# Eight-core two-layer hybrid backbone: second layer's conditioning pieces later, tokens in chained pieces, unread matmuls in all planned waits

## The chip, the cores and the metric

The kernel runs on the 8 cores of one Trainium2 chip. All cores run the same program, each on its own share of the tokens, with the same weights, and no core talks to another. The time is the device time of the slowest core in microseconds (us). Each core has TensorE (matmuls), VectorE, ScalarE, GpSimd and SyncE; DMAs are issued from GpSimd's queue (the pool queue) and from SyncE's.

## What is computed

Two layers over 2048 tokens a core: 1024 context tokens (4 sequences of 256) and 1024 latent tokens (one sequence). Layer 0 mixes with a bidirectional RG-LRU (a gated linear recurrence), layer 1 with a chunked token-mixing MLP; each is followed by a SwiGLU FFN (1024 to 2816 to 1024). Every norm is modulated by a shift and a scale, and every branch by a gate, computed from a conditioning vector:

```python
def adaln(cond, w, b):
    m = jax.nn.silu(cond) @ w + b          # w: (1024, 6 * 1024) per layer
    return m.reshape(cond.shape[0], N_MOD, D_MODEL)

for i in range(DEPTH):
    hp = rmsnorm(xp, norm_mix[i]) * (1.0 + mp[:, 1]) + mp[:, 0]
    op = mixer(hp)                          # RG-LRU in layer 0, chunk MLP in layer 1
    xp = xp + mp[:, 2] * op
    hp = rmsnorm(xp, norm_ffn[i]) * (1.0 + mp[:, 4]) + mp[:, 3]
    xp = xp + mp[:, 5] * swiglu(hp, ...)    # and the same for the latent tokens with ms
```

## The kernel before

**Tiling.** Tokens stand as columns, features on the partitions, in four tiles of 512 tokens: tiles 0 and 1 are context, 2 and 3 latent. A matmul is 128 x 128 weights against 512 tokens; eight of them over the 1024 features fill one PSUM bank. PSUM has 8 banks: `BF` hands out 0 to 3 in turn, `BM` 4 to 6, and bank 7 gathers the conditioning.

**The planner.** The program is first recorded as tasks (`Prog._add`, line 163) with an engine, a priority (lower goes first), a planned duration, the tasks that they depend on, and for DMAs a planned rate. `Prog.schedule` (line 211) is a list scheduler that simulates the five engines and writes one fixed order for each. `slack` is added to a task's planned end, so what depends on it is planned later; it costs nothing by itself. On the chip each engine goes through its list strictly in order, with semaphore waits where a task depends on another engine's: a matmul whose data are late holds up all that stand behind it. ScalarE's choice (line 236) adds a penalty for a task whose function needs another activation table: `SWP` = 12 for tasks with priority 1 or more, `URG` = 2 for those below.

**Unread matmuls.** `Prog.warm` (line 268) goes through the planned order of TensorE; in each planned gap of over 0.8 us that begins before `WARM` = 400 us it puts up to ten matmuls of 256 columns (`onesB` against `condT`), whose result nobody reads, into a free bank. They show in the trace as `pb<-condT,onesB`.

**Order of the work.** x tile 0 and layer 0's conditioning are loaded; `lru((0,))` is the recurrence of tile 0 over 8 chunks of 128 features, `out_proj` its output projection; then the FFN's group 0 for tile 0 runs interleaved with `lru((1,))` (priority `P1`), whose projection follows (`out_proj(0, ..., (1,), sp=OSP1)`: the first `sp` of 8 chunk matmuls of a bank as one task, the rest as another, so the first can go before the last chunks are done). While tile 1 is worked on, the space of x tiles 2 and 3 holds recurrence weights; afterwards both tiles are loaded (`load_x`, 2 MB each, on SyncE's queue), normed into h, and their space serves `lru((2, 3))` as scratch; behind it they are loaded again, in eight quarter loads on the pool queue (`XRP` = 3), for the residual of `out_proj` of tiles 2 and 3. Meanwhile `ffn(0, 0)` does FFN group 0 for tile 1, then groups 1 and 2 for tiles 0 and 1, at the lowest priority 5: it fills TensorE whenever nothing else is ready. Then come `ffn(0, 1)`, layer 1, and the final norms.

**FFN and conditioning pieces.** `ffn` (line 619) goes through groups of the 22 hidden chunks (8, 8, 6). For each pair of chunks it loads a gate and an up weight (1 MB each, read as f32, stored as bf16) through the four slots of `ringF`, and then four down weights. `mods` is a list of conditioning pieces: after each pair and after each down weight one is taken from it, with its load through the next slot of `ringF`. A piece (`mod_piece`, line 452) is 1 MB of weights (`modw`; layer 0's last ones come as `modc`) and four matmuls against `condT` into bank 7; after the last piece of a set `mod_final` transposes the sum and writes modT and amod, which norms and residuals read. Layer 0's later pieces are planned with 2 us of slack (`SLK`), layer 1's with none. `ffn(0, 0)` for tile 1 carries layer 1's first set (8 pieces), `ffn(0, 1)` the other 16.

Projection weights and `lru_in` pieces go through the three slots of `ringM`.

Of the kernel before, what the change touches and what calls it, by code (L numbers as in the profile page):

```python
# [13 lines left out]
KC = 8  # L14
# [121 lines left out]
SLK, URG = 2.0, 2.0  # L136
PN = 0
OSP, OSP1 = 6, 8
# [4 lines left out]
M4 = 0  # L143
XRP = 3
# [3 lines left out]
P1 = 0.8  # L148
# [4 lines left out]
WARM = 400.0  # L153
PRE = (5, 6, 9, 9, 4, 4, 4, 6)
TABLE_US = 1.28
# [196 lines left out]
def snapshot(ress):  # L352
    out = set()
    for r in ress:
        if r.w is not None:
            out.add(r.w)
        out.update(r.r)
    return list(out)
# [21 lines left out]
def emit_program(P, A):  # L380
# [71 lines left out]
    def mod_piece(l, G, kc, prio=None, ring=ringF):  # L452
# [6 lines left out]
        wv, wres = ring.load(desc, 1 << 20, prio=prio, slack=SLK if l == 0 and G > 0 else 0.0)  # L459
# [51 lines left out]
    def load_x(tt, extra=()):  # L511
        P.dma("sp", "xs%d" % tt, lambda e: e.dma_start(out=x_fm[:, tt], in_=A["d_xin"][tt]),
              wr=[XR[(m, tt)] for m in range(KC)], extra=extra, nbytes=2 << 20)

# [104 lines left out]
    def ffn(l, hf, extra=(), mods=(), ep=1, after=None, segs=((0, (0, 1)), (1, (0, 1)), (2, (0, 1))), kept=None):  # L619
# [16 lines left out]
        for grp, tls in segs:  # L636
            j0, j1 = FGROUPS[grp]
            nj = j1 - j0
            for jp in range(j0, j1, 2):
# [26 lines left out]
                if mods:  # L666
                    mod_piece(*mods.pop(0), prio=2)
# [18 lines left out]
            if last and tls == (1,):  # L686
                last_tile(2 * hf + 1, [dload(pi) for pi in range(4)], nj, BZ)
            else:
                for pi in range(4):
                    down(pi, tls, *dload(pi))  # L690
                    if mods:
                        mod_piece(*mods.pop(0), prio=2)
                if last:
                    after(2 * hf)
# [94 lines left out]
    GK6 = Res()  # L789
# [392 lines left out]
    load_x(2, extra=snapshot(KR[0:3] + [GK6]))  # L1182
    load_x(3, extra=snapshot(LR[4].all() if M4 else KR[3:6] + [GK6]))
# [11 lines left out]
    for tt in (2, 3):  # L1195
        if XRP == 0:
            load_x(tt, extra=xre)
            continue
        for q in range(4):
            P.dma("pool", "xq%d" % (4 * (tt - 2) + q), lambda e: e.dma_start(out=x_fm[:, tt, 2 * q:2 * q + 2, :], in_=A["d_xin"][tt][:, 2 * q:2 * q + 2, :]),  # L1200
                  wr=[XR[(2 * q, tt)], XR[(2 * q + 1, tt)]], extra=xre, nbytes=1 << 19, prio=XRP)
# [4 lines left out]
    ffn(0, 0, segs=((0, (1,)), (1, (0, 1)), (2, (0, 1))) if NSEG == 1 else ((0, (1,)), (1, (1,)), (2, (0, 1))), mods=[(1, 0, kc) for kc in range(KC)])  # L1206
# [198 lines left out]
```

How the kernel before makes its waits and increments, by code:

```python
    def then_inc(self, sem, n):  # L49
        self.call.append((sem, n))
        return self
# [57 lines left out]
    "dma_start": lambda e, a, k: e.dma_start(*a, **k),  # L109
    "matmul": lambda e, a, k: e.matmul(*a, **k),
    "memset": lambda e, a, k: e.memset(*a, **k),
    "scalar_tensor_tensor": lambda e, a, k: e.scalar_tensor_tensor(*a, **k),
    "tensor_copy": lambda e, a, k: e.tensor_copy(*a, **k),
    "tensor_reduce": lambda e, a, k: e.tensor_reduce(*a, **k),
    "tensor_scalar": lambda e, a, k: e.tensor_scalar(*a, **k),
    "tensor_tensor": lambda e, a, k: e.tensor_tensor(*a, **k),
    "tensor_tensor_scan": lambda e, a, k: e.tensor_tensor_scan(*a, **k),
    "transpose": lambda e, a, k: e.transpose(*a, **k),
    "wait_ge": lambda e, a, k: e.wait_ge(*a, **k),
}
def replay(calls, e):
    for c in calls:
        ins = PLAY[c[0]](e, c[1], c[2])
        for (sem, n) in c[3:]:
            ins.then_inc(sem, n)
# [187 lines left out]
    def emit(self, order, sems, dsems):  # L314
# [22 lines left out]
                        kn[k2] = v2  # L337
                if kn.get(key, 0) < val:
                    kn[key] = val
            if t.dsem is not None:
                dcount[t.dsem] += 16
                t.tok = (t.dsem, dcount[t.dsem])
                t.last.then_inc(dsems[t.dsem], 16)
            else:
                count[e] += 1
                t.tok = (e, count[e])
                t.last.then_inc(sems[e], 1)
            t.know = dict(kn)
            q[e].append(t.calls)
        return q
```

## Time and profile before

| | |
|---|---|
| time, median of 3 runs | 1532.39 us (1531.67 to 1532.84) |
| the profiled execution | 1532.15 us, span of its slowest core (6) 1530.6 us |
| spans of cores 0 to 7 | 1517.4, 1529.7, 1529.6, 1517.4, 1529.7, 1516.5, 1530.6, 1517.2 us |
| mean granted TensorE clock of the cores | 0.983 to 0.989 |
| busy, share of the span | TensorE 94%, VectorE 59%, ScalarE 43%, GpSimd 15% |
| DMA | 151.56 MB, mean busy share of the 16 engines on the pool queue 53.2%, on SyncE's 3.4% |
| chain that ended last | TensorE 79%, DMA 9%, ScalarE 5%, issue 4%, VectorE 3% |

All rows below are of core 6. Times are microseconds from the span's start. PE is TensorE's matmuls, PEld its weight loads, DVE VectorE, ACT ScalarE, POOL GpSimd, SPq SyncE's queue. `out<-in` names what an instruction writes and reads: `pb` is PSUM, `h` the normed tokens, `MS` the recurrence's output, `FS` the FFN's hidden part, `x_fm` the tokens, and `condT` the conditioning vectors. Most operations are recorded by one helper, so that their line (L110, L105, ...) says only their kind. In brackets behind an instruction stands the time that its engine was idle before it, and what ended that. Matmuls are pipelined, so a mean of 380 ns is the time of one from start to end; eight in a row take 1.73 us.

### The profile page before, as it was taken

The numbers are of one execution on the slowest core, as the hardware profiler recorded it, in microseconds if no ns is written. First come the engines' busy times: TensorE is split into PE (matmuls) and PEld (weight loads), VectorE is DVE, ScalarE is ACT, GpSimd is POOL, SyncE is SP. The second block draws the span as 40 slices with busy tenths as digits, with TensorE's granted clock in tenths as the row PEclk, the third lists the DMA queues.
The fourth block names the chain that finished last, engine by engine and source line by source line (L and its number), as shares of the span: only waits on it lengthen the run. The fifth ranks groups of instructions, "written<-read, shape, count | busy, mean of one in ns | idle before, by whom it ended". The sixth has DMA issues, their size and how long they took to land.

```text
span 1530.6 us, 20044 instructions; the slowest of 8 cores (1516.5 to 1530.6 us)
## 1 busy us (share of the span) xinstructions
PE 1437.0 (94%) x6971; PEld 661.7 (43%) x6971; DVE 906.6 (59%) x1316; ACT 650.6 (43%) x866; POOL 225.7 (15%) x377
## 2 busy tenths in 40 slices
PE   4978996899999999999999999999999999999997
PEld 2433443444444445444444444444444444444444
DVE  1578695458687646528863364538856447744446
ACT  2597996548888234632013032632125013201023
POOL 6011021135231210011111100011110000101000
PEclk9999998999999999999999999999999999999999
DMA  9998368499435873554646754353332535985303
GB/s 176 171 191 129 49 110 193 57 156 146 74 60 86 168 137 55 84 83 70 110 69 97 117 101 72 56 83 56 55 63 47 86 55 93 198 142 87 65 1 110
DMA packets 50182, 151.56 MB, mean 99 GB/s; under 512 B 5410, under 2 KB 11042, under 8 KB 49572
## 3 DMA queue, kind: packets, MB, share of 16 engines
q0 software_dynamic: 45312, 133.32, 53.2%
q1 hardware_dynamic: 4772, 16.96, 3.4%
q8 instruction: 58, 0.95, 0.3%
q14 instruction: 40, 0.33, 0.1%
HBM read 270.94 MB, written 8.42 MB: 183 GB/s over the span
## 4 chain that ended last, share of the span: by engine, by line
PE 79%; DMA 9%; ACT 5%; issue 4%; DVE 3%; POOL 0%; DVEq 0%; ACTq 0%; POOLq 0%
PE pb L110 78%; DMA ringF<-modw 4%; DMA x_fm<-lru_in 2%; ACT h L105 1%; ACT reg L105 1%; ACT L105 1%; DMA x_fm<-xin 1%; DMA ringM<-lru_in 1%; DMA ringF<-ffn_d 1%; DVE x_fm L112 1%; DVE tmpn L112 1%; DMA tff<-lru_w_out 0%; ACT FS L105 0%; ACT x_fm L105 0%; DMA ringM<-lru_w_out 0%
## 5 line engine op out<-in xcount | busy, mean ns | idle before, releaser
L110 PE MATMUL pb<-h,ringF 128*128 128x512 bf16 x2624 | 585.7, 380 | 1.8 <-DVE FS L116 0.9
L110 PEld LDWEIGHTS pb<-h,ringF 128*128 128x128 bf16 x2624 | 255.3, 98 | 311.6 <-issue 9.3
L112 DVE SCALAR_TENSOR_TENSOR x_fm<-pb,modT,x_fm 128x512 f32<-128x512 f32 (+1 forms) x264 | 192.5, 733 | 196.6 <-PE pb L110 191.1
L110 PE MATMUL pb<-FS,ringF 128*128 128x512 bf16 x1312 | 296.6, 383 | 5.0 <-DVE x_fm L112 2.4
L105 ACT ACTIVATE tff<-pb 128x512 f32<-128x512 f32 x176 | 104.8, 596 | 385.7 <-PE pb L110 385.4
L112 DVE SCALAR_TENSOR_TENSOR tff<-tff,pb 128x512 f32<-128x512 f32 x176 | 120.2, 685 | 167.4 <-ACT tff L105 167.3
L110 PEld LDWEIGHTS pb<-FS,ringF 128*128 128x128 bf16 x1312 | 128.5, 99 | 161.8 <-issue 14.5
L116 DVE TENSOR_TENSOR FS<-tff,pb 128x512 bf16<-128x512 f32 x176 | 120.4, 685 | 68.8 <-PE pb L110 65.9
L105 ACT ACTIVATE h<-x_fm 128x1024 bf16<-128x1024 f32 (+2 forms) x86 | 84.2, 994 | 141.0 <-DVE x_fm L112 134.8
L105 ACT ACT_TABLE_LOAD x84 | 107.8, 1283 | 76.9 <-PE pb L110 69.3
L110 PE MATMUL pb<-h,ringM 128*128 128x512 bf16 x548 | 124.1, 380 | 4.3 <-DMA ringM<-lru_in 3.3
L105 ACT ACTIVATE reg<-reg 128x1024 f32<-128x1024 f32 (+1 forms) x68 | 57.4, 855 | 122.9 <-DVE reg L116 108.2
L110 PE MATMUL pb<-MS,ringM 128*128 128x512 bf16 x472 | 105.5, 379 | 3.7 <-DMA ringM<-lru_w_out 2.2
L105 ACT ACTIVATE h<-tmpn,modT 128x512 bf16<-128x512 f32 x120 | 82.4, 716 | 56.7 <-DVE tmpn L112 55.3
L112 DVE SCALAR_TENSOR_TENSOR tmpn<-x_fm,amod,rstd 128x512 f32<-128x512 f32 x120 | 86.2, 747 | 16.4 <-ACT rstd L105 8.9
L110 PEld LDWEIGHTS pb<-h,ringM 128*128 128x128 bf16 x548 | 53.3, 98 | 70.2 <-issue 7.2
L110 PEld LDWEIGHTS pb<-MS,ringM 128*128 128x128 bf16 x472 | 45.7, 98 | 60.4 <-issue 6.7
L109 POOL DMA_DIRECT2D ringF<-ffn_g x45 | 24.6, 548 | 265.5 <-PE pb L110 265.1
L110 PE MATMUL pb<-reg,h 128*128 128x512 bf16 x256 | 60.2, 379 | 0.0
L109 POOL DMA_DIRECT2D ringF<-ffn_d x48 | 25.7, 536 | 222.6 <-PE pb L110 218.3
L116 DVE TENSOR_TENSOR reg<-reg 128x1024 f32<-128x1024 f32 (+1 forms) x48 | 52.8, 1108 | 6.5 <-ACT reg L105 5.9
L110 PE MATMUL pb<-h,x_fm 128*128 128x512 bf16 x212 | 51.0, 379 | 5.6 <-ACT h L105 2.6
(152 smaller groups left out, 1252.3 us busy)
## 6 DMA issues: line engine op xcount, KB each, us to landing
ringF<-ffn_g POOLq DMA_DIRECT2D x45, 512.0 KB, 5.7
ringF<-ffn_u POOLq DMA_DIRECT2D x45, 512.0 KB, 6.9
ringF<-ffn_d POOLq DMA_DIRECT2D x36, 512.0 KB, 7.1
ringF<-modw POOLq DMA_DIRECT2D x34, 512.0 KB, 8.1
x_fm<-xin SPq DMA_DIRECT2D x4, 2048.0 KB, 14.3
yout<-x_fm SPq DMA_DIRECT2D x12, 512.0 KB, 8.3
ringM<-lru_in POOLq DMA_DIRECT2D x20, 256.0 KB, 5.6
ringM<-lru_w_out POOLq DMA_DIRECT2D x19, 256.0 KB, 5.7
```

What stands on the lines that cost most here:

```text
L105: "activation": lambda e, a, k: e.activation(*a, **k),
L109: "dma_start": lambda e, a, k: e.dma_start(*a, **k),
L110: "matmul": lambda e, a, k: e.matmul(*a, **k),
L112: "scalar_tensor_tensor": lambda e, a, k: e.scalar_tensor_tensor(*a, **k),
L116: "tensor_tensor": lambda e, a, k: e.tensor_tensor(*a, **k),
```

## The change

Six settings and two places in the program change:

- `mfrom=MF` with MF = 1: `ffn(0, 0)` takes no conditioning pieces in group 0 and begins with them in group 1. `ffn(0, 1)` is as before.
- Layer 1's pieces are planned with `SL1` = 3 us of slack, where they had none.
- `OSP1` = 6, before 8: tile 1's output projection is split in 6 + 2 chunk matmuls.
- `P1` = 1.0, before 0.8: the priority of `lru((1,))`. No other task lies between the two numbers, but ScalarE's penalty for a change of table becomes 12 there, before 2.
- `X4` = 3: x tiles 2 and 3 are loaded both times by `load_x4` on SyncE's queue, in quarters of 512 KB, each of which waits for the one before to have landed; the quarters of tile 3 follow those of tile 2.
- `WARM` = 9e9: unread matmuls go into planned gaps of the whole program.

```diff
-OSP, OSP1 = 6, 8
+OSP, OSP1 = 6, 6
-P1 = 0.8
+P1 = 1.0
-WARM = 400.0
+WARM = 9e9
+MF, SL1 = 1, 3.0
+X4 = 3
@@ mod_piece
-        wv, wres = ring.load(desc, 1 << 20, prio=prio, slack=SLK if l == 0 and G > 0 else 0.0)
+        wv, wres = ring.load(desc, 1 << 20, prio=prio, slack=SL1 if l == 1 else SLK if G > 0 else 0.0)
@@ emit_program
+    def load_x4(tts, extra=()):
+        prev = list(extra)
+        for tt in tts:
+            for q in range(4):
+                t = P.dma("sp", "xs%d" % tt, lambda e: e.dma_start(out=x_fm[:, tt, 2 * q:2 * q + 2, :], in_=A["d_xin"][tt][:, 2 * q:2 * q + 2, :]),
+                          wr=[XR[(2 * q, tt)], XR[(2 * q + 1, tt)]], extra=prev, nbytes=1 << 19)
+                prev = [t]
@@ ffn, at both places
-                if mods:
+                if mods and grp >= mfrom:
                     mod_piece(*mods.pop(0), prio=2)
@@ first load of tiles 2 and 3
-        load_x(2, extra=snapshot(KR[0:3] + [GK6]))
-        load_x(3, extra=snapshot(LR[4].all() if M4 else KR[3:6] + [GK6]))
+        load_x4((2,), snapshot(KR[0:3] + [GK6]))
+        load_x4((3,), snapshot(LR[4].all() if M4 else KR[3:6] + [GK6]) + [P.tasks[-1]])
@@ second load of tiles 2 and 3
-        for q in range(4):
-            P.dma("pool", "xq%d" % (4 * (tt - 2) + q), lambda e: e.dma_start(...), wr=[...], extra=xre, nbytes=1 << 19, prio=XRP)
+        load_x4((2, 3), xre)
@@ second part of the FFN of tiles 0 and 1
-    ffn(0, 0, segs=..., mods=[(1, 0, kc) for kc in range(KC)])
+    ffn(0, 0, segs=..., mods=[(1, 0, kc) for kc in range(KC)], mfrom=MF)
```

## Rows read from the trace of the kernel before

**Rows 1.** The page, section 1: busy us, share of the span, instructions.

```profile
PE 1437.0 (94%) x6971; PEld 661.7 (43%) x6971; DVE 906.6 (59%) x1316; ACT 650.6 (43%) x866; POOL 225.7 (15%) x377
```

**Rows 2.** TensorE's waits, whole span: us in total, times, longest.

```profile
PE pb L110 <- DMA ringF<-modw: 21.0, 10, 14.7
PE pb L110 <- DMA MS<-modw: 17.4, 3, 15.8
...
PE pb L110 <- DMA ringM<-lru_w_out: 2.2, 2, 1.5
PE pb L110 <- DMA ringF<-ffn_d: 2.2, 1, 2.2
```

**Rows 3.** Windows: us, busy (instructions) per engine, granted clock, DMA share, GB/s.

```profile
243.00:260.00 17.00, 2.27 (x18) 1.31 (x17) 9.47 (x17) 8.00 (x9) 0.53 (x1) 0.66 1.03 217
260.00:283.00 23.00, 20.80 (x105) 10.45 (x104) 5.25 (x7) 9.56 (x10) 4.10 (x8) 0.95 0.68 106
283.00:297.00 14.00, 9.56 (x56) 5.46 (x55) 7.28 (x11) 8.22 (x12) 0.68 (x2) 0.88 0.29 39
297.00:345.00 48.00, 46.75 (x221) 20.35 (x222) 25.93 (x39) 26.03 (x41) 14.43 (x24) 1.00 0.81 128
```

**Rows 4.** TensorE in order of time, 239 to 268: start, us, instruction, idle before.

```profile
243.20 1.26 PE L110 MATMUL pb<-condT,onesB 128*128 128x256 bf16 x10
259.19 0.62 PE L110 MATMUL pb<-ringF,condT 128*32 128x512 bf16 x4 [14.73 <-DMA ringF<-modw]
259.74 3.94 PE L110 MATMUL pb<-condT,onesB 128*128 128x256 bf16 x24
263.52 1.89 PE L110 MATMUL pb<-h,onesB 128*128 128x512 bf16 x8
265.25 2.97 PE L110 MATMUL pb<-MS,ringM 128*128 128x512 bf16 x13
```

**Rows 5.** GpSimd in order of time: the request of 240.24.

```profile
240.24 0.53 POOL L109 DMA_DIRECT2D ringF<-modw  x1 [3.14 <-PE pb L110]
```

**Rows 6.** TensorE in order of time: the statistics after 624.

```profile
624.49 3.63 PE L110 MATMUL pb<-h,onesB 128*128 128x512 bf16 x16
```

**Rows 7.** VectorE in order of time: the last write of MS.

```profile
252.28 0.69 DVE L116 TENSOR_TENSOR MS<-reg,MS 128x512 bf16<-128x512 f32 x1
```

**Rows 8.** DMA issues from 230 to 260: KB each, median us to landing.

```profile
ringM<-lru_w_out POOLq DMA_DIRECT2D x2, 256.0 KB, 19.1
```

**Rows 9.** Windows behind 400, columns as in rows 3.

```profile
400.00:450.00 50.00, 47.52 (x221) 21.41 (x220) 37.19 (x40) 41.97 (x54) 18.38 (x18) 1.00 0.43 71
...
480.00:500.00 20.00, 17.12 (x76) 7.32 (x75) 15.15 (x15) 18.38 (x24) 2.12 (x5) 0.94 0.56 93
...
870.00:890.00 20.00, 16.33 (x74) 7.16 (x73) 6.74 (x13) 0.00 (x0) 2.74 (x6) 0.91 0.93 164
1300.00:1320.00 20.00, 17.80 (x75) 7.61 (x74) 17.22 (x24) 8.78 (x12) 2.65 (x5) 0.91 0.89 157
```

**Rows 10.** TensorE's waits from 300 to 900: total, times, longest.

```profile
PE pb L110 <- DMA ringF<-modw: 4.2, 6, 1.6
```

**Rows 11.** The two token loads issued at 230.5 and 230.9: time to landing.

```profile
DMA to landing us min/median/max: 12.0/16.8/21.6
```

**Rows 12.** DMA issues from 260 to 283.

```profile
ringM<-lru_w_out POOLq DMA_DIRECT2D x5, 256.0 KB, 4.6
```

**Rows 13.** DMA issues of the whole span: KB each, median us to landing.

```profile
yout<-x_fm SPq DMA_DIRECT2D x12, 512.0 KB, 8.3
...
x_fm<-xin POOLq DMA_DIRECT2D x8, 512.0 KB, 18.9
```

**Rows 14.** ScalarE's groups from 145 to 255: count, busy us, mean ns, idle before.

```profile
L105 ACT ACT_TABLE_LOAD x24 | 30.8, 1283 | 1.1 <-PE pb L110 0.5
```

**Rows 15.** The window 145 to 255, columns as in rows 3.

```profile
145.00:255.00 110.00, 95.01 (x469) 44.16 (x469) 85.39 (x144) 99.20 (x121) 16.30 (x28) 0.97 0.56 111
```

**Rows 16.** The group of unread matmuls, whole span: count, busy us, mean ns.

```profile
L110 PE MATMUL pb<-condT,onesB 128*128 128x256 bf16 x316 | 46.4, 292 | 7.3 <-ACT h L105 4.1 <-ACT MS L105 1.9 <-DVE modT L116 0.7
```

More of the change, by code:

```diff
@@ L617, in emit_program, with ffn @@
     BM = Banks([4, 5, 6])
-    def ffn(l, hf, extra=(), mods=(), ep=1, after=None, segs=((0, (0, 1)), (1, (0, 1)), (2, (0, 1))), kept=None):
+    def ffn(l, hf, extra=(), mods=(), ep=1, after=None, segs=((0, (0, 1)), (1, (0, 1)), (2, (0, 1))), kept=None, mfrom=0):
         mods = list(mods)
@@ L690, in ffn @@
                     down(pi, tls, *dload(pi))
-                    if mods:
+                    if mods and grp >= mfrom:
                         mod_piece(*mods.pop(0), prio=2)
@@ L1181, in emit_program @@
     P.prio = 1
-    load_x(2, extra=snapshot(KR[0:3] + [GK6]))
-    load_x(3, extra=snapshot(LR[4].all() if M4 else KR[3:6] + [GK6]))
+    if X4 & 1:
+        load_x4((2,), snapshot(KR[0:3] + [GK6]))
+        load_x4((3,), snapshot(LR[4].all() if M4 else KR[3:6] + [GK6]) + [P.tasks[-1]])
+    else:
+        load_x(2, extra=snapshot(KR[0:3] + [GK6]))
+        load_x(3, extra=snapshot(LR[4].all() if M4 else KR[3:6] + [GK6]))
     P.prio = PB
@@ L1194, in emit_program @@
     xre = snapshot(LR[5].all() + LR[6].all() + GWB)
[L1195 to L1198, printed above, removed]
-        for q in range(4):
-            P.dma("pool", "xq%d" % (4 * (tt - 2) + q), lambda e: e.dma_start(out=x_fm[:, tt, 2 * q:2 * q + 2, :], in_=A["d_xin"][tt][:, 2 * q:2 * q + 2, :]),
-                  wr=[XR[(2 * q, tt)], XR[(2 * q + 1, tt)]], extra=xre, nbytes=1 << 19, prio=XRP)
+    if X4 & 2:
+        load_x4((2, 3), xre)
+    else:
+        for tt in (2, 3):
+            if XRP == 0:
+                load_x(tt, extra=xre)
+                continue
+            for q in range(4):
+                P.dma("pool", "xq%d" % (4 * (tt - 2) + q), lambda e: e.dma_start(out=x_fm[:, tt, 2 * q:2 * q + 2, :], in_=A["d_xin"][tt][:, 2 * q:2 * q + 2, :]),
+                      wr=[XR[(2 * q, tt)], XR[(2 * q + 1, tt)]], extra=xre, nbytes=1 << 19, prio=XRP)
     out_proj(0, "d_lru_w_out", (2, 3), BM, ringM)
@@ L1205, in emit_program @@
     cm_setup(BM)
-    ffn(0, 0, segs=((0, (1,)), (1, (0, 1)), (2, (0, 1))) if NSEG == 1 else ((0, (1,)), (1, (1,)), (2, (0, 1))), mods=[(1, 0, kc) for kc in range(KC)])
+    ffn(0, 0, segs=((0, (1,)), (1, (0, 1)), (2, (0, 1))) if NSEG == 1 else ((0, (1,)), (1, (1,)), (2, (0, 1))), mods=[(1, 0, kc) for kc in range(KC)], mfrom=MF)
     ffn(0, 1, mods=[(1, G, kc) for G in (1, 2) for kc in range(KC)])
```

## The prediction

> **What bounds the kernel now.** I read the page first [rows 1]: TensorE is busy for 1437.0 us, 94% of the 1530.6 us span, no other engine for more than 59%. So the time is TensorE's work plus TensorE's idle time, and only two things can shorten it: less idle time (93.6 us) or a higher clock in the stretches where it was granted less than full. The list of TensorE's waits [rows 2] splits the idle time by cause: 17.4 us at the start for the first conditioning pieces (not touched), then 21.0 us for conditioning pieces in ringF, of which one wait alone is 14.7 us; the rest is many waits of 1 to 2 us. A table of windows [rows 3] puts that wait in place: from 243 to 260 TensorE is busy 2.27 of 17 us and the granted clock is 0.66 (a mean of the two levels, 1.2 and 2.4 GHz), while the DMA engines are full (1.03). From 297 on it is nearly full again (46.75 of 48 us). The order of TensorE's instructions there [rows 4] shows whose fault it is: ten unread matmuls at 243.20, nothing until 259.19, then four matmuls of a conditioning piece (ringF against condT), 24 more unread ones, statistics, and at 265.25 the output projection of token tile 1. The piece was requested at 240.24 [rows 5] and is of modw, not modc; layer 0's last pieces are all modc, so this is one of the second layer's first eight, whose first reader is the norm at 624.49 [rows 6]. It blocks the engine because its four matmuls were planned here and the engine takes its list in order.
>
> **Part 1, the second layer's first eight pieces later (mfrom=1, slack 3).** Eight groups of four matmuls and eight 1 MB reads leave group 0 of the FFN and go to group 1; none is removed. The wait of 14.73 us [rows 4] goes. What is late next? The projection needs the last chunk of the recurrence, written by VectorE at 252.28 + 0.69 = 252.97 [rows 7]. So the projection can start at 253.1 + 1.73 for the statistics that stood ahead of it (263.52 to 265.25) = 254.9 instead of 265.25: -10.4 us, at most -12.1 if the statistics lie in the wait. Its weights have to be there too: the two requested from 230 to 260 took 19.1 us to land [rows 8], the second, requested right behind the piece, until 260; the piece's own 1 MB was ahead of it in the pool queue, and its removal brings it forward. The matmuls of the moved pieces (0.4 us each) cost the same in their new place. That place is under the scans of tiles 2 and 3: four with the gate and up weights of group 1, where the DMA is busy 0.43 (400 to 450), and four with its down weights, up to about 525, where it is 0.56 and more [rows 9], against 0.81 where most of them stood (297 to 345, [rows 3]). They must be through by the norm at 624.49 [rows 6], and are with 100 us to spare.
>
> The second layer's pieces were planned with no slack. From 300 on TensorE waits 4.2 us for them, the longest 1.6 [rows 10], so that 3 us of planned slack covers each. I take -2.5, bounds -4 and +2 (a slot freed 3 us later makes the weight behind it later; there is one such wait today, for ffn_d, 2.2 us [rows 2]).
>
> **Part 2, OSP1 8 to 6.** The projection of tile 1 is cut in 6 + 2 chunk matmuls. The three weights that the ring holds allow 18 matmuls of 1.73 / 8 = 0.216 us, 3.9 us, of work before 253.0, two of them 2.6 us. Against that stands that weights arrive late. I take -1.5, bounds -3.9 and 0. Nothing is added but eight planned groups.
>
> **Part 3, tokens in chained pieces.** The two 2 MB loads issued at 230.5 landed after 12.0 and 21.6 us [rows 11]; beside them a projection weight took 19.1 us [rows 8], against 4.6 us after 260 [rows 12]. Chained, at most 0.5 MB of them is in flight. A piece takes at least 12.0/4 = 3.0 us, at most the 8.3 us that a 512 KB output store took [rows 13]; eight take 24 to 66 us. I take 4.8 each (nearer to the fast end, which is the same kind of load), 38 us, so tile 3 lands at about 269 and not 252. Good: the pool queue gets more until 252. Bad: from 253 to 269 the projection's eight weights (1.73 us of TensorE each) share with the tokens. Alone, three slots at 4.6 + 1.73 us gave 2.1 us a weight and 2.2 us of waits [rows 2]; at 7 us (between 4.6 and 19.1, nearer to the first, as only a quarter is in flight) it is 2.9 us. For the five weights not yet loaded: 5 x 0.8 = +4, bounds 0 and +8.
> A rule of the Trainium skill speaks against this part. The trace shows 2 MB in 12.0 us at the fastest, and nothing of its fixed part [rows 11]. "DMA: Bandwidth & Descriptors" (Measured; Anatomy of one DMA) says that a DMA costs about 2 us whatever its size and that DMAs should be batched to 1 MiB or more; here no run shows a chained piece. By it the eight pieces would cost 16 us more than two transfers, an end at 268, which would leave the sum as it is.
> The second reload (before: eight requests on the pool queue from 516 on, landing after 18.9 us in the median [rows 13]) becomes 38 us of chain, until some 555; TensorE has FFN matmuls of tiles 0 and 1 to put between the projections until the norm at 624.49 [rows 6], 70 us later. So 0; bounds -1 and +5 (the 5 of a chain that is late for one projection bank after another). The pool queue also loses eight instructions of about 0.5 us each, behind which a weight stood.
>
> **Part 4, ScalarE's order (P1 0.8 to 1.0).** Lower than 1, a change of table counted 2 in ScalarE's plan; now it counts 12 in the recurrence of tile 1 also, so changes are batched. From 145 to 255 ScalarE is busy 99.2 of 110 us, and 24 table loads of 1.283 us are 30.8 of it [rows 14, 15]: three for each of the eight chunks. This stretch ends with the chunk that now sets 253.0. A quarter fewer would be 7.7 us. But batching delays single chunks, and TensorE is idle there for 110 - 95.01 = 15 us [rows 15], 10.5 of it in the wait of part 1 (which begins at 244.5), so that 4.5 us of waits and an unread matmul here and there are to be won, and then the wait for the last chunk. I take -4, bounds -10 and +8.
>
> **Part 5, unread matmuls in all planned waits (WARM).** 316 are there today, all before 367 us [rows 16]. Of the places after 400 with the clock below 1.00 [rows 9], 480 to 500 (0.94, over 17.1 busy us), 870 to 890 (0.91, 16.3) and 1300 to 1320 (0.91, 17.8) lose 1.0 + 1.5 + 1.6 = 4.1 us. Of the curable 4.1 us I take a little over half, 2.4; against it stand fillers of 256 / 2.4 = 107 ns each that delay work where a planned wait isn't there: ten groups of some five are 5 us, mostly in true waits, 1.4 charged. -1, bounds -4 and +5.
>
> **Clock of the stretch 243 to 297.** 0.66 over 2.3 us, 0.95 over 20.8, 0.88 over 9.6 busy us [rows 3] lose 0.8 + 1.0 + 1.2 = 3.0 us; with a wait of 9 us left I take half: -1.5.
>
> **Sum** (against the profiled execution, 1532.15 us, span 1530.6; the median of the three runs is 1532.39): -10.4 - 2.5 - 1.5 + 4 + 0 - 4 - 1 - 1.5 = -16.9 us, so 1515.5 us by the median. The cores' spans fall in two groups (about 1517 and 1530 us); all rows are of the slowest, core 6, which sets the time.
>
> **Rivals.**
> 1. *The gain goes to the projection's weights and the scan.* Tokens still landing at 253 to 290 at the pool queue's expense (waits +8), tables and split no help (0), slack, fillers and clock 1 us each: -10.4 + 8 - 3 = -5.4, 1527. For it: the 19.1 us landings beside the token loads [rows 8]. Against: those were two unchained 2 MB.
> 2. *The token chain ends too late.* At 8.3 us a piece tile 3 lands at 297; with a norm like the one from 283 to 297 [rows 3] the scans of tiles 2 and 3 start at 311, when FFN work of tile 1, which starts at 285 now, has been alone for 26 us. Each pair of its weights (2 MB read) feeds only 32 matmuls, 6.9 us, and the DMA is at 0.81 today with the scans' matmuls between [rows 3]: alone it would starve a quarter of the time, some 7 us. 1515.5 + 7 = 1522. For it: the store's 8.3 us. Against: the load's 3.0 us a piece.
> 3. *Slower: batched tables hold up the recurrence of tile 1.* A chunk's Sqrt waits behind FFN Tanh and other chunks, at most the 12 us that the plan allows. If the last chunk comes later than 265.2 (12.2 us after 252.97), all of -10.4 is gone; from there each us costs one. With 8 us more, and the rest of the sum at -1: 1532.4 + 8 - 1 = 1539. For it: VectorE is also at 85.4 of 110 us [rows 15] and scans wait for Sqrt. Against: the plan sees this chain, and FFN Tanh shares its table with the recurrence's Tanh and Exp.
> 4. *Much faster*: the tables bring -10 and the weights cost nothing: 1505.
> 5. *It doesn't do what it says*: the eight pieces have a later place in the code, but the plan puts another prefetch of equal harm there (the slot takes an FFN weight). An FFN weight's matmuls are not due before the norm at 297, so I give it 0.03, at 1531.
>
> **How the numbers follow.** Forecast 0.60 (own range 1508 to 1523), rival 1 0.14, rival 2 0.09, rival 3 0.06, rival 4 0.08, rival 5 0.03. Range for 8 in 10: 1504 to 1529. 0.2% is 3.1 us, about what a measurement of this kernel can tell from no change. Faster: forecast, rivals 2 and 4, most of 1: 0.87. Same: the slow end of rival 1 and rival 5: 0.07. Slower: 0.06.
>
> **What would show it.** Right: no modw wait above 2 us after 40 us; windows from the end of tile 0's FFN to tile 1's projection with less than 9 us idle; the projection starting within 2 us of the last chunk's write; fewer than 24 table loads in tile 1's recurrence; token pieces landing in 4 to 6 us; DMA share of 400 to 500 above 0.5 with no new wait; clock above 0.97 at the norms. Wrong: waits for lru_w_out over 6 us, a wait for DVE or ACT before tiles 2 and 3, TensorE idle after 515, or more fillers with no higher clock.

## The result, and the profile after

| | before | after |
|---|---|---|
| median of the runs beside each other | 1533.41 us | 1541.75 us |
| ratio, 95% interval | | 1.005 [1.0035, 1.0065] |
| span of the slowest core in the profile | 1530.6 us | 1538.0 us (core 5) |
| mean span of the 8 cores | 1523.5 us | 1531.2 us |

The forecast was 1515.5 us, within 1504 to 1529: wrong, and on the wrong side. The change makes the kernel slower by 8 us, where 17 us less had been worked out. Each median is over six executions of which one was in a slower state (1789 us before, 1711 us after), which the ratio leaves out. The page of after, sections 1 and 6 (queue, count, size, median us to landing), against [rows 1, 13]:

```profile
PE 1447.0 (94%) x7007; PEld 663.8 (43%) x7007; DVE 904.9 (59%) x1316; ACT 647.4 (42%) x864; POOL 217.0 (14%) x369
...
x_fm<-xin SPq DMA_DIRECT2D x16, 512.0 KB, 5.0
```

TensorE's waits over the whole span of after (total, times, longest), against [rows 2]:

```profile
PE pb L110 <- DMA MS<-modw: 16.3, 2, 15.7
PE pb L110 <- DMA ringM<-lru_w_out: 15.3, 5, 7.5
...
PE pb L110 <- DVE x_fm L112: 7.2, 6, 2.2
PE pb L110 <- DMA ringF<-modw: 2.5, 3, 1.3
```

The wait for conditioning pieces did go, from 21.0 to 2.5 us. But the projection's weights (`lru_w_out`) now cost 15.3 us where they cost 2.2. TensorE from 245 on shows where, against [rows 4]; a projection matmul is `pb<-MS,ringM`:

```profile
245.84 1.26 PE L110 MATMUL pb<-condT,onesB 128*128 128x256 bf16 x10
254.57 2.72 PE L110 MATMUL pb<-MS,ringM 128*128 128x512 bf16 x6 [7.48 <-DMA ringM<-lru_w_out]
257.08 2.87 PE L110 MATMUL pb<-h,onesB 128*128 128x512 bf16 x8
259.79 1.69 PE L110 MATMUL pb<-condT,onesB 128*128 128x256 bf16 x14
261.32 1.46 PE L110 MATMUL pb<-MS,ringM 128*128 128x512 bf16 x6
262.61 1.25 PE L110 MATMUL pb<-condT,onesB 128*128 128x256 bf16 x10
267.99 5.93 PE L110 MATMUL pb<-MS,ringM 128*128 128x512 bf16 x16 [4.13 <-DMA ringM<-lru_w_out]
...
281.37 1.89 PE L110 MATMUL pb<-MS,ringM 128*128 128x512 bf16 x8 [3.07 <-DMA ringM<-lru_w_out]
...
296.39 3.79 PE L110 MATMUL pb<-h,ringF 128*128 128x512 bf16 x9 [0.28 <-ACT h L105]
```

The idle time has only been cut into three. The FFN of tile 1 (`pb<-h,ringF`) starts at 296.39; before it started at 296.94, the end of the third window of [rows 3]. So by 297 nothing is won and nothing lost on these cores, and the 7.4 us by which the span grew come later. They are there at the norm that opens layer 1, at 624.49 before [rows 6] and here in after:

```profile
631.00 3.62 PE L110 MATMUL pb<-h,onesB 128*128 128x512 bf16 x16
```

It is not idle time of that last stretch: from 515 to 632 TensorE has one wait, of 2.2 us, and before it had 1.3 us. It is work that had been done earlier in before and is now left over. Windows with the matmuls that read ringF alone (the FFN's, and the four of each conditioning piece: 28 and 4 of the counts in before, 32 in the first window of after; columns: us, busy, count, granted clock, DMA share, GB/s), before first, then after:

```profile
297.00:510.00 213.00, 126.17 (x564) 0.99 0.62 99
510.00:570.00 60.00, 30.89 (x138) 1.00 0.87 175
570.00:630.00 60.00, 48.30 (x214) 0.94 0.45 73
```

```profile
297.00:510.00 213.00, 123.09 (x551) 0.99 0.62 99
510.00:570.00 60.00, 26.60 (x112) 0.94 0.79 165
570.00:630.00 60.00, 52.84 (x236) 0.97 0.46 74
```

Up to 570 after has done 7.4 us less of this work (3.08 + 4.29), 41 matmuls of the FFN's own, and behind 570, when the latent tiles' projection is over and only the FFN is left ahead of the norm, it pays for it.

**A table by stage.** One core is not enough for differences of a few us, so I took for each kernel the mean over its 8 cores of five points in TensorE's order: the first FFN matmul of tile 1 (A), the first projection matmul of tiles 2 and 3 (B), the statistics after it (C), those of layer 1's first norm (D), and TensorE's last instruction (E). "Last chunk" is the mean start of VectorE's last write of MS for tile 1 ([rows 7] has core 6). All in us from the start.

| kernel | last chunk | A | B | C | D | A to D | E |
|---|---|---|---|---|---|---|---|
| before | 251.5 | 295.7 | 513.2 | 565.5 | 620.0 | 324.3 | 1516.1 |
| after | 257.9 | 294.1 | 510.1 | 566.1 | 628.3 | 334.2 | 1522.8 |
| a4 (only unread matmuls) | 253.5 | 298.6 | 516.7 | 568.7 | 622.7 | 324.1 | 1519.5 |
| a2 (only split) | 253.6 | 299.7 | 517.0 | 569.7 | 623.9 | 324.2 | 1520.3 |
| a1 (only pieces) | 253.2 | 292.0 | 509.1 | 561.6 | 625.4 | 333.4 | 1520.2 |
| b3 (two places later) | 252.8 | 291.4 | 506.2 | 562.8 | 614.3 | 322.9 | 1508.1 |
| b2 (second chain) | 253.1 | 297.7 | 515.0 | 573.5 | 628.0 | 330.3 | 1527.0 |
| b4 (changed, no chain) | 257.6 | 297.2 | 514.0 | 569.1 | 633.9 | 336.7 | 1527.0 |
| c2 (only P1) | 256.8 | 294.9 | 511.8 | 563.9 | 617.6 | 322.7 | 1513.7 |
| d2 (no split, no chain) | 257.0 | 290.9 | 508.3 | 562.3 | 626.7 | 335.8 | 1520.3 |

Kernels of one letter ran together on one chip. Between letters, and against the profiles of before and after, the same kernel differs by some 3 us (the kernel before had a median of 1536.2 us beside the a kernels, 1535.1, 1538.1 and 1533.2 beside b, c and d; a4, with nothing changed ahead of A but unread matmuls, reaches it 2.9 us later than before). Durations within a kernel and differences inside a letter are what to read.

**Where A to D is lost.** Between A and D every kernel does the same 867 FFN matmuls (counted in the traces). What differs is how many of them are done under the scans, that is from A to B. Means of the 8 cores, us:

| | before | a4 | a1 | after | b3 | c4 | c3 |
|---|---|---|---|---|---|---|---|
| A to B | 217.5 | 218.1 | 217.1 | 216.0 | 214.8 | 217.2 | 215.6 |
| FFN matmuls done in it | 556 | 556 | 525 | 525 | 556 | 517 | 556 |
| TensorE idle in it | 6.3 | 6.0 | 13.3 | 8.5 | 5.2 | 12.7 | 4.1 |
| unread matmuls in it | 9 | 17 | 0 | 40 | 4 | 0 | 22 |
| B to D | 106.8 | 106.0 | 116.3 | 118.2 | 108.1 | 113.8 | 113.4 |
| TensorE idle in it | 0.6 | 0.3 | 3.0 | 3.6 | 1.7 | 0.2 | 5.4 |

A to B takes 215 to 218 us whether 556 or 517 FFN matmuls fill it. Fewer of them do not make it shorter: TensorE idles instead (a1, c4), or runs unread matmuls and idles (after). The work left over comes behind B and makes B to D longer. In after 3.0 of the 3.6 us of idle time behind B are waits for the residual add, which the second chain causes (b2 below), and in a1 2.7 of 3.0 us are waits for FFN down weights.

### The profile page after: what moved, and what is told of

Same layout as the page of the kernel before. It is cut to its first block, busy times and chain, and to the rows that moved or that the text cites. A ratio compares the mean times of both kernels' runs of the same rounds, so it can differ in the third digit from the quotient of the medians.

```text
span 1538.0 us, 20150 instructions; the slowest of 8 cores (1526.2 to 1538.0 us)
## 1 busy us (share of the span) xinstructions
PE 1447.0 (94%) x7007; PEld 663.8 (43%) x7007; DVE 904.9 (59%) x1316; ACT 647.4 (42%) x864; POOL 217.0 (14%) x369
## 4 chain that ended last, share of the span: by engine, by line
PE 81%; DMA 7%; ACT 4%; issue 4%; DVE 3%; POOL 1%; DVEq 0%; ACTq 0%; POOLq 0%; SPq 0%
PE pb L110 81%; DMA ringF<-modw 2%; DMA ringM<-lru_w_out 1%; DMA ringF<-ffn_u 1%; ACT h L105 1%; ACT reg L105 1%; POOL reg L115 1%; ACT L105 1%; DVE x_fm L112 1%; DMA x_fm<-xin 1%; DMA ringF<-ffn_d 1%; DMA ringM<-lru_in 1%; ACT FS L105 0%; DVE rstd L114 0%; DVE tmpn L112 0%
## 5 line engine op out<-in xcount | busy, mean ns | idle before, releaser
L110 PE MATMUL pb<-MS,ringM 128*128 128x512 bf16 x472 | 111.0, 393 | 18.6 <-DMA ringM<-lru_w_out 15.3
L112 DVE SCALAR_TENSOR_TENSOR tmpn<-x_fm,amod,rstd 128x512 f32<-128x512 f32 x120 | 86.2, 746 | 18.3 <-ACT rstd L105 11.6
L105 ACT ACTIVATE reg<-pb,dcol 128x512 f32<-128x512 f32 x80 | 50.7, 684 | 16.8 <-PE pb L110 16.6
L116 DVE TENSOR_TENSOR reg<-reg 128x1024 f32<-128x1024 f32 (+1 forms) x48 | 52.7, 1107 | 8.4 <-ACT reg L105 7.8
```

The lines of the kernel that those rows point to most:

```text
L105: "activation": lambda e, a, k: e.activation(*a, **k),
L110: "matmul": lambda e, a, k: e.matmul(*a, **k),
L112: "scalar_tensor_tensor": lambda e, a, k: e.scalar_tensor_tensor(*a, **k),
L116: "tensor_tensor": lambda e, a, k: e.tensor_tensor(*a, **k),
```

## The experiments

Sixteen kernels. Ratios are against the kernel before on the same chip, with the 95% interval.

| run | ratio | | run | ratio |
|---|---|---|---|---|
| a1 only pieces | 1.0012 [0.9998, 1.0025] | | c1 pieces + split | 1.0042 [1.0015, 1.0069] |
| a2 only split | 0.9997 [0.9985, 1.0009] | | c2 only P1 | 0.9949 [0.9912, 0.9985] |
| a3 only chains | 1.0069 [1.0046, 1.0093] | | c3 changed, two later | 1.0002 [0.9975, 1.0029] |
| a4 only unread | 0.9999 [0.9985, 1.0013] | | c4 two later, slack 4 | 0.9978 [0.9947, 1.0009] |
| b1 first chain | 1.0028 [1.0012, 1.0045] | | d1 changed, no split | 1.0067 [1.0040, 1.0094] |
| b2 second chain | 1.0045 [1.0032, 1.0057] | | d2 no split, no chain | 1.0022 [1.0012, 1.0032] |
| b3 two later | 0.9941 [0.9921, 0.9960] | | d3 two later + P1 | 0.9944 [0.9923, 0.9966] |
| b4 changed, no chain | 1.0050 [1.0030, 1.0069] | | d4 d3 + unread | 0.9931 [0.9907, 0.9956] |

**One part at a time (a1 to a4).** Each is the kernel before with one part of the change:

```diff
a1:  +MF, SL1 = 1, 3.0      (and its two places in mod_piece and ffn)
a2:  -OSP, OSP1 = 6, 8      +OSP, OSP1 = 6, 6
a3:  +X4 = 3                (and load_x4 at both loads)
a4:  -WARM = 400.0          +WARM = 9e9
```

> The kernel before with the later conditioning pieces (mfrom=1, slack 3) and nothing else of the change. Theory A (the pieces push FFN weights out of the four ring slots under the scans of tiles 2 and 3, so that less FFN work lies in front of the projection of tiles 2 and 3): the 14.7 us wait at 243 is gone and the FFN of tile 1 starts 8 to 12 us earlier, but in TensorE's order 728 instead of 760 FFN matmuls stand ahead of that projection, and the 32 missing ones (6.9 us) and more are paid after it: ratio 0.997 to 1.002, 1528 to 1536 us. Rival theory B (the pieces are harmless, and the chained tokens or the unread matmuls took the gain): the full gain of 12 to 15 us, 1518 to 1521 us.

The part that was to bring 13 us brings nothing. TensorE in a1:

```profile
253.81 1.89 PE L110 MATMUL pb<-h,onesB 128*128 128x512 bf16 x8 [0.28 <-ACT h L105]
255.62 1.89 PE L110 MATMUL pb<-MS,ringM 128*128 128x512 bf16 x8
263.46 5.35 PE L110 MATMUL pb<-MS,ringM 128*128 128x512 bf16 x16 [5.96 <-DMA ringM<-lru_w_out]
```

The projection starts at 255.62, within 1 us of the 254.9 that the prediction worked out. Then the second weight is not there, for 5.96 us. GpSimd's requests in a1 show that the place in the queue did not stay empty:

```profile
242.60 0.53 POOL L109 DMA_DIRECT2D ringF<-ffn_g  x1 [3.14 <-PE pb L110]
243.12 0.54 POOL L109 DMA_DIRECT2D ringM<-lru_w_out  x1
```

Where the conditioning piece had been requested just ahead of this weight [rows 5], an FFN gate weight of the same 1 MB now is, and the two token loads are in flight as before. A is reached 6.6 us earlier than in a4. But from A to D a1 takes 333.4 us where a4 takes 324.1: 9.3 us are given back. Two of the waits in which they go, one just ahead of the projection of tiles 2 and 3, where no FFN matmul is left to fill it, and one behind, for an FFN down weight:

```profile
511.39 3.57 PE L110 MATMUL pb<-FS,ringF 128*128 128x512 bf16 x8 [7.03 <-DVE x_fm L112]
...
527.47 6.46 PE L110 MATMUL pb<-FS,ringF 128*128 128x512 bf16 x16 [3.20 <-DMA ringF<-ffn_d]
```

> The kernel before with the projection of tile 1 split in 6 + 2 chunk matmuls (OSP1=6) and nothing else. Theory C (the first parts of three rows take all three weight slots and keep them until the last chunk is there, so that the other weights are requested only then): the requests for the fourth and later lru_w_out weights come in one bunch, with over 5 us of waits for lru_w_out against 2.2, and no gain or a loss of 1 to 4 us: 1533 to 1537 us. Rival (the split gives work in the wait, as I predicted): 1.5 to 4 us faster, 1529 to 1531 us.

No effect alone: the piece's wait hides whatever it does.

> The kernel before with both token loads in chained quarter pieces (X4=3) and nothing else. If the chain relieves the pool queue from 230 on, the modw wait at 243 shrinks from 14.7 us to some 8 us and the time by 3 to 7 us: 1526 to 1530 us. If the chain is what costs (theory B), the second reload makes the projection of tiles 2 and 3 wait for tokens: over 3 us more waits for VectorE's x_fm after 515, and 1535 to 1540 us.

The dearest part alone, 0.69%. TensorE in a3:

```profile
250.71 3.30 PE L110 MATMUL pb<-condT,onesB 128*128 128x256 bf16 x17
262.65 3.57 PE L110 MATMUL pb<-h,onesB 128*128 128x512 bf16 x8 [8.64 <-ACT h L105]
266.02 5.83 PE L110 MATMUL pb<-MS,ringM 128*128 128x512 bf16 x23
```

The statistics of the first latent tile (`pb<-h,onesB`) stand ahead of the projection in TensorE's order, and they need all of the tile, squared by ScalarE. Chained, the tokens come later, and the projection, whose data are there, waits behind the statistics. The prediction had counted these as 1.73 us of work and not as a wait.

> The kernel before with unread matmuls in all planned waits (WARM) and nothing else: 31 more of them, 3.3 us of matmul time. If the planned waits are real on the chip: within 1 us of before, 1532 to 1534 us, with a higher clock in 480 to 515 or 1300 to 1320. If they stand where there is no wait (theory B's second half): 2 to 3.5 us slower, 1535 to 1537 us.

Nothing, with 31 more unread matmuls in the program's order. It also serves as the unchanged kernel of its chip.

**The two chains apart, the pieces elsewhere, the change without the chains (b1 to b4).**

```diff
b1:  +X4 = 1       b2:  +X4 = 2       b4 (the changed kernel):  -X4 = 3   +X4 = 0
b3 (a1, but the list of pieces moved by two places instead of to the next group):
+MF, SL1 = 2, 3.0
@@ ffn, against the kernel before; the last five lines at both places
+        if mfrom:
+            mods = [None] * mfrom + mods
-                if mods:
-                    mod_piece(*mods.pop(0), prio=2)
+                pc = mods.pop(0) if mods else None
+                if pc is not None:
+                    mod_piece(*pc, prio=2)
```

> The kernel before with only the first load of token tiles 2 and 3 chained (X4=1). In the run with both chains the FFN of tile 1 started 3.7 us later than in the run with only the unread matmuls added, because the statistics of tile 2 stand in TensorE's list ahead of the projection of tile 1 and waited 8.6 us for the tokens. If that is the cause: FFN of tile 1 3 to 5 us later, nothing lost at 515 to 570, ratio 1.002 to 1.004. If the first chain is harmless and the second one is all: ratio 1.000 plus or minus 0.001.

> The kernel before with only the second load of token tiles 2 and 3 chained (X4=2); TensorE's order has the same FFN matmuls in the same places. In the run with both chains the stretch from the first matmul of the projection of tiles 2 and 3 to their statistics took 58.2 us, against 52.0. If the second chain does that (the projection's banks wait for the late quarters): 5 to 7 us there and ratio 1.003 to 1.005, with nothing before 515. Rival: the longer stretch is an after-effect of the first chain, ratio 1.000 plus or minus 0.001.

Both cost, 0.28% and 0.45%, and together they make a3's 0.69%. In b2 B to C takes 58.5 us, in a4, a2, a1 and before 52.0 to 52.7: the projection waits for VectorE's residual add and that for a late quarter, three waits of 3.19 us and less. SyncE's queue in b2 (start, us from first to last, count) and TensorE:

```profile
517.30 51.01 SPq L109 DMA_DIRECT2D x_fm<-xin  x8
```

```profile
528.27 6.46 PE L110 MATMUL pb<-MS,ringM 128*128 128x512 bf16 x16 [3.19 <-DVE x_fm L112]
```

Eight pieces take 51 us from the first issue to the last, where the prediction had 38 us, landing included, and its cost at 0.

> The kernel before with the eight conditioning pieces two places later in the same list (the first after the third pair of group 0, the last after the second pair of group 1), slack 3, nothing else of the change. In TensorE's order 760 FFN matmuls stand ahead of the projection of tiles 2 and 3, as before, and 880 up to its end (864 before, 816 in the run with the pieces in group 1). Theory A (the wait's gain is real, and only the displaced FFN work takes it back): FFN of tile 1 6 to 8 us earlier as in that run, the stretch after the statistics at 565 not longer, ratio 0.993 to 0.996, 1523 to 1530 us. Rival (whatever is won before 297 is lost in the scans of tiles 2 and 3, which their own chain of ScalarE and VectorE sets): ratio 0.999 to 1.001.

This is the run that settles most. The first pieces leave the same place, the same wait goes, the weights are as late (a wait of 5.33 us in the place of a1's 5.96), and A is within 1 us of a1's (291.4 and 292.0, another chip). Yet the kernel is 0.6% faster, since A to D takes 322.9 us and not 333.4. Where the pieces are put matters more than that they leave. The programs say why. Counted in the order in which each kernel hands TensorE its matmuls (fixed when the kernel is built), FFN matmuls that stand ahead of the first and the last projection matmul of tiles 2 and 3 (a count of the built programs by operand gives 8 fewer in every cell; the differences, on which the argument rests, are the same):

| | before, a2, a4 | b3 | c3 | a1 | c4 | after |
|---|---|---|---|---|---|---|
| ahead of the first | 760 | 760 | 760 | 728 | 720 | 728 |
| ahead of the last | 864 | 880 | 864 | 816 | 824 | 824 |
| A to D, us | 324 | 322.9 | 329.1 | 333.4 | 331.0 | 334.2 |

So 32 to 48 FFN matmuls, 7 to 10 us at 0.216 us each, slip behind the projection in a1 and after, and the traces have the first 32 of them (525 done from A to B and not 556). My reading of why the planner does this is that in group 1 the eight pieces take slots of ringF, each for its load, its four matmuls and 3 us of planned slack, while the scans of tiles 2 and 3 run, so that FFN weights come later. That reading is argued and not shown. Nor is the place alone what decides: built and counted on the table's basis, but not run, the pieces in their old place with 3 us of slack give 712 and 800, in group 1 without slack 720 and 816, two places later without slack 728 and 848. Place and slack together turn the order, and no simple rule for it comes out of these counts.

> The changed kernel without the chained loads (X4=0); all else of the change is in it. If the chains cost what they cost alone (0.7%), this is 8 to 11 us faster than the changed kernel: ratio 0.997 to 0.999 against the kernel before. If in the changed kernel their cost is mostly hidden, because tile 1's projection is late there for other reasons: ratio 1.002 to 1.005.

The changed kernel without its chains is as slow as with them (1.0050 both), although they cost 0.69% alone. TensorE in b4:

```profile
259.67 5.28 PE L110 MATMUL pb<-MS,ringM 128*128 128x512 bf16 x12 [12.76 <-DMA ringM<-lru_w_out]
```

With the unchained token loads back, the third weight, which one of the three first parts needs, is late by 12.76 us. The chains had cut this to 7.48 (after, above). Behind B b4 waits 3.6 us for FFN down weights in the mean of the cores, where after waits 3.0 us for the residual add.

**The order of the FFN, the split and the priority (c1 to c4).**

```diff
c1:  a1 with OSP1 = 6          c2 (before):  -P1 = 0.8   +P1 = 1.0
c3:  the changed kernel with b3's two places
c4:  b3 with   -MF, SL1 = 2, 3.0    +MF, SL1 = 2, 4.0
```

> The kernel before with the later pieces and the 6 + 2 split of tile 1's projection (mfrom=1, slack 3, OSP1=6), no chain, no other part. With the pieces alone the projection of tile 1 ended at 278.8 and the FFN of tile 1 began at 292.0 (means of the eight cores). Theory C (the three first parts keep the three weight slots until the last chunk, and a first part waits for the third weight, which is late beside the token loads): FFN of tile 1 at 296 to 298, waits for lru_w_out over 12 us, ratio 1.004 to 1.006. If the split is neutral, as it was alone: as with the pieces alone, 1.000 to 1.0025.

The split, free alone, costs once the pieces' wait is gone: A at 298.2 where a1 has 292.0 (the chips differ; by the ratios it is 0.3%, 4.6 us, though their intervals overlap). On c1's own chip c4, which has the wait gone and no split, reaches A at 289.9. GpSimd's requests in after show how:

```profile
237.55 0.53 POOL L109 DMA_DIRECT2D ringM<-lru_w_out  x1 [2.92 <-PE pb L110]
...
244.98 0.54 POOL L109 DMA_DIRECT2D ringM<-lru_w_out  x1
262.45 1.59 POOL L109 DMA_DIRECT2D ringM<-lru_w_out  x3 [16.94 <-PE pb L110]
```

Three weights have done their first six matmuls and stay in their slots until the last two chunks are there. So for 17 us nothing is requested, and then three at once, which TensorE waits for at 267.99 and behind. In a1 the requests stand at 258.05 and 267.58, one by one.

> The kernel before with ScalarE's switch penalty of the recurrence of tile 1 at 12 in place of 2 (P1=1.0), nothing else. My prediction gave it -4 us for fewer table loads. In the changed kernel only 2 of 84 table loads went, so now I expect 0 to -2 us, ratio 0.998 to 1.001, since the wait for the conditioning piece at 243 sets the end of that stretch anyway.

> The changed kernel in all its parts, except that the eight pieces stand two places later in the list of ffn(0, 0), not eight (no mfrom). Its order has 760 and 864 FFN matmuls ahead of the start and the end of the projection of tiles 2 and 3, like the kernel before; the changed kernel has 728 and 824. Theory A: the 40 matmuls (8.6 us) come back, 7 to 10 us faster than the changed kernel, ratio 0.998 to 1.000. If the displacement is not what costs in the changed kernel: ratio 1.004 to 1.006.

The changed kernel with b3's places loses half a per cent less than it did and is level with before: A to D 329.1 and not 334.2. It is not all of b3's gain, since chains and split stay: of the 5.4 us that TensorE idles behind B, 5.0 are waits for the residual add.

> The kernel with the pieces two places later (0.994 with 3 us of planned slack), with one number changed: 4 us of planned slack. Same loads, same matmuls; but the planner's order now has 720 and 824 FFN matmuls ahead of the start and the end of the projection of tiles 2 and 3, not 760 and 880. Theory A: 40 to 56 matmuls of 0.216 us are exposed behind that projection, 8 to 11 us more: ratio 0.999 to 1.002, with the stretch from the statistics at 565 to the norm at 620 some 8 to 12 us longer. If the place of the FFN work doesn't count, because TensorE is idle for its waits in any order: 0.993 to 0.996.

One us more of planned slack, with no other edit, takes 40 FFN matmuls from ahead of the projection and makes A to D 331.0 and not 322.9 (E is 6.4 us later, on another chip). By the ratios, 0.9978 and 0.9941, the loss is 5.7 us and the intervals overlap at their edge; by stages it is clear, and it goes with the order in b3, c3, a1 and after alike. The order is thus the cause, whatever turns it. The missing matmuls can be seen under the scans, where TensorE is busy 5.9 us less and for 45 matmuls fewer, c4 first, then b3 (columns as in [rows 3]):

```profile
300.00:500.00 200.00, 189.34 (x877) 83.36 (x875) 142.19 (x153) 153.65 (x198) 65.46 (x76) 0.98 0.64 103
```

```profile
300.00:500.00 200.00, 195.19 (x922) 86.64 (x920) 149.56 (x162) 157.66 (x202) 68.41 (x83) 1.00 0.64 104
```

**Do split and chain stand in for each other, and what is best (d1 to d4).**

```diff
d1 (the changed kernel):  -OSP, OSP1 = 6, 6   +OSP, OSP1 = 6, 8
d2 (d1):                  -X4 = 3             +X4 = 0
d3 (b3):                  -P1 = 0.8           +P1 = 1.0
d4 (d3):                  -WARM = 400.0       +WARM = 9e9
```

> The changed kernel with the projection of tile 1 unsplit (OSP1=8), chained loads kept. Theory D (chain and split stand in for each other: without the split the statistics of tile 2 stand ahead of the projection and wait for the chained tokens, with it they stand behind three first parts, and it is the weights that are late): a wait of TensorE for ScalarE's h of 5 us or more near 255, FFN of tile 1 within 2 us of the changed kernel, ratio 1.004 to 1.008. If the split is a cost of its own in the changed kernel: 3 us or more faster than the changed kernel, 1.000 to 1.003.

> The changed kernel with neither split nor chain; left of the change are the pieces in group 1 with slack 3, P1 and the unread matmuls. Theory D: only without both is the gain ahead of 297 there, FFN of tile 1 at 290 to 293, and what is left against the kernel before is that gain minus the displaced FFN work: ratio 0.998 to 1.001. If chain and split don't matter inside the changed kernel: 1.004 to 1.006.

Without the split the changed kernel is no faster (1.0067), without both it is (1.0022 [1.0012, 1.0032]), by more than either alone. In d1 TensorE waits 2.37 us for the chained tile's squares ahead of the statistics and 4.91 us for a weight; in d2 its longest wait for a weight there is 0.8 us and A is at 290.9, the best of the table. What d2 keeps is the FFN's order: A to D is 335.8.

> The kernel before with the pieces two places later, slack 3 (0.994 alone) and P1=1.0 (0.995 alone, interval 0.991 to 0.9985). If both gains are real and apart: 0.989 to 0.992. Both act on the stretch that ends with tile 1's projection; if P1's gain was the smaller wait for the piece at 243, which is gone here, or chance: 0.993 to 0.995.

> As d3, and unread matmuls in all planned waits (WARM). Alone they gave 0.9999. If they are neutral here too: within 0.1% of d3. If some 40 more of them delay work now that TensorE runs closer to its plan: 0.1 to 0.3% slower than d3.

P1 adds nothing to b3 that can be seen, nor do the unread matmuls to that. All three lie at 0.993 to 0.994; d4's median is 1522.23 us beside 1533.23 of before, the fastest kernel of this study.

## Why the prediction was wrong

**Part 1, the wait (-10.4).** The mechanism was right and the size was half wrong. The wait went in every kernel with the edit, and the projection could start where it was said. What is late next was named too (the weights), with the claim that the piece's removal "brings it forward". It did not: the requests beside the token loads took 18.4 us in a1 (19.1 before [rows 8]). The plan put an FFN weight of the same size in the piece's place in the queue, so a1 does not tell the piece from the tokens; after and d1 do, where the tokens are chained, a 1 MB FFN weight is also just ahead, and the weights land in 7.9 and 9.2 us. Measured by A: -6.6 us, and -7.7 with d2, where no weight was late by more than 0.8 us (290.9 against a4's 298.6, measured apart).

**Part 1, "cost the same in their new place": the step that failed.** I had priced eight moved pieces by their matmuls and by the DMA share at the new place [rows 9], and read the FFN as filler that loses nothing by standing aside. But the pieces also take ring slots, and the order is planned ahead: 32 FFN matmuls slipped out of the time under the scans, where TensorE then idles 7.3 us more (a1 against a4), and had to be done between the projection and the norm of 624.49, where nothing else is left. Price +9.3 us, measured in a1 (B to D is 10.3 us longer than in a4: 6.9 are the 32 matmuls, 2.7 more idle time), undone in b3 (-10.5 us on A to D) and in part in c3 (-5.1); it is more than the whole gain of the wait. The condition that decides stood in the prediction ("must be through by the norm at 624.49") as a thing with 100 us to spare. The pieces have that; the FFN has none: TensorE is nearly full from 300 to the norm (6.9 us idle from A to D in before), and A to B does not shrink when FFN matmuls leave it, so each that leaves costs its 0.216 us behind B.

**The slack (-2.5).** The waits for pieces from 300 to 900 went from 4.2 us [rows 10] to none, yet slack is not free, as the description of the planner and the prediction held it to be: c4 loses some 6 to 8 us by one us of it. It is free on the chip and has a price in the plan. No run has the moved pieces without slack.

**Part 2, the split (-1.5).** Wrong sign: 0 alone, about +5 beside the moved pieces. "The three weights that the ring holds allow 18 matmuls" was true of the slots and not of the landings, and I hadn't asked when a slot comes free: a slot held for a half-done weight requests nothing.

**Part 3, the chains (+4 and 0).** The first cost 0.28%, 4.3 us, as the sum had it (+4), but that is luck, since the reason was another: not through the weights of the projection but through statistics that stand ahead of it in TensorE's order (the longest wait for ScalarE's h is 5.9 us in b1). The second cost 0.45%, 7 us, where I took 0 with +5 as its bound. A piece was taken at 4.8 us; the median was 5.0 to 6.6, but from one issue to the next it was 7.3 us in the mean (51.01 us for seven steps in b2). That TensorE "has FFN matmuls of tiles 0 and 1 to put between the projections" failed on the order again: nothing is put between at run time. The last piece of the first chain was issued at 274.2 in after, where I had all of tile 3 landed at about 269. In the changed kernel both costs are covered, since without the chains the projection's weights are later, and FFN down weights are late behind B (b4).

**Part 4, tables (-4).** Its premise failed. From 145 to 255 ScalarE loads as many tables as before [rows 14]:

```profile
L105 ACT ACT_TABLE_LOAD x24 | 30.8, 1283 | 1.9 <-PE pb L110 1.2
```

What the setting does is rival 3's mechanism in small. VectorE's last write of MS in c2:

```profile
258.55 0.69 DVE L116 TENSOR_TENSOR MS<-reg,MS 128x512 bf16<-128x512 f32 x1
```

In the mean of the cores the last chunk is written at 256.8 to 258.0 in all eight kernels with P1 = 1 and at 251.5 to 255.5 in all ten of those without it, against [rows 7]; the chunk before it comes some 3 us earlier. That is 4 us of the 12.2 at which rival 3 would have decided, and it never reached TensorE: in c2 the piece's wait covers it, in d3 the projection starts at 257.7 and not at b3's 254.5 but finds its weights landed, and ends earlier (277.1 and 278.2). c2's ratio of 0.9949 has a wide interval, and by stages its gain of some 2 us lies within what chips differ by. Whether P1 alone gains stays open; on top of b3 it does not.

**Part 5, unread matmuls (-1).** Within its bounds, and zero. They did raise the clock: the three places of [rows 9] are all at 1.00 in after (in a4 the first two are, the third stays at 0.91). After:

```profile
480.00:500.00 20.00, 18.79 (x100) 8.18 (x99) 15.41 (x15) 19.29 (x24) 3.70 (x7) 1.00 0.81 137
870.00:890.00 20.00, 19.03 (x100) 8.60 (x99) 7.50 (x10) 0.00 (x0) 2.53 (x5) 1.00 1.00 167
1300.00:1320.00 20.00, 17.79 (x84) 7.96 (x82) 18.72 (x26) 10.52 (x13) 2.64 (x5) 1.00 0.79 137
```

That the fillers themselves take what it gains is likely and not shown.

**The clock of 243 to 297 (-1.5).** It got worse and not better. In after it was 0.80 over 9.5 busy us, 0.85 over 15.2 and 0.99 over 9.8 in the three windows of [rows 3], which lose 1.9 + 2.3 + 0.1 = 4.3 us where before lost 3.0. The single wait of 14.7 us had become three, with work between them.

**The sum again, as measured:** pieces -6.6 to A and +9.3 behind it, split about +5 (which includes what it does to the clock there), chains and P1 on top about 0 (b4 and after have one ratio, 1.0050), unread 0: +8, beside the 8.3 us between the medians. The terms of split and chains depend on each other (d1, d2), so this sum holds in this order only.

**The rivals.** Rival 1 (weights) had its place right: a1 and b3 wait 5 to 6 us for them and after 15.3. Rival 2 had a late first chain that holds up the scans and starves the FFN; the chain was late, though less than that (its last piece was issued at 274.2; rival 2 has tile 3 landed at 297), but A to B is no longer than before (216.0 and 217.5 us), so its mechanism did not show. What b2 shows is the second chain, for which I had only the +5 of part 3. Rival 3's 1539 us is the nearest number, and its mechanism gave 4 of the 12.2 us that it needed. Rival 5, "another prefetch of equal harm", had its mechanism right: an FFN weight took the piece's place in the queue, and the projection's weight stayed late behind it. Its price was not the one that decided. No rival had the cost as work that slips behind a deadline, and that is why 94% of my chances lay at or below no change. What I had written as signs of being wrong, "waits for lru_w_out over 6 us", came true.

## What to carry to other kernels

Where an engine is full up to a deadline, fillers are not free to move: before a prefetch is moved under a long stage, count what it displaces from there (slots as well as matmuls), and put it down at the price of that work behind the stage. In a kernel whose order is planned ahead, small planned numbers (a place, a us of slack) can cost more than what they cure; try two or three neighbours of such a setting before judging the idea, as the same idea was worth -0.6% at one place (b3) and nothing at the next (a1, 1.0012 [0.9998, 1.0025]). An edit that is neutral alone may only be hidden by the wait that another edit removes.

## What the runs showed of the hardware

- A chained 512 KB quarter on SyncE's queue took 3.8 us at its fastest, 5.0 to 6.6 in the median, while the faster of two unchained 2 MB loads in flight together took 12.0 us [rows 11], 3.0 for a quarter: so 0.8 us more at the fastest. The Trainium skill ("DMA: Bandwidth & Descriptors", Anatomy of one DMA) gives about 2 us for what a DMA costs whatever its size, in a fit for DMAs that GpSimd issues; neither the trace of before nor these runs isolate it on SyncE's queue, and at the fastest it shows as less. By that figure eight pieces carry six more such costs than two loads do, an estimate of 12 us and not the 16 of the prediction.
- The token loads slow the pool queue's requests, and chaining them helps: the `lru_w_out` requests of 230 to 260 took 18.3 to 19.1 us in before, a1 and b3 and 16.0 and 15.8 us in d2 and b4, all with two 2 MB loads in flight, and 7.9 and 9.2 us in after and d1, where the tokens are chained. In all of them 1 MB reads for FFN or conditioning weights stood around them in the same queue, so none shows the weights without these.
- A higher granted clock in a few short windows did not show in the time: in a4 the windows 480 to 500 and 870 to 890 stand at 1.00 (0.94 and 0.91 in [rows 9]), and its ratio is 0.9999 [0.9985, 1.0013].
